# Up units in feature form: the low-weight and high-weight products issued in turns, tile by tile, instead of in two runs of eight

## The reference, cut to what matters

```python
def squared_relu_mlp(hn, w_up, w_down):
    return jnp.square(jax.nn.relu(hn @ w_up)) @ w_down
...
        h = h + squared_relu_mlp(rmsnorm(h, mlp_norm_g[i]), mlp_w_up[i], mlp_w_down[i])
...
        hf = _rms_norm(x, norm_ffn_pre[l])
        u = _dwconv_causal(hf @ w_up[l], ffn_dw[l]) + ffn_dw_b[l]
        u_g, u_v = jnp.split(u, 2, axis=-1)
        yff = (jax.nn.silu(u_g) * u_v) @ w_down[l]
```

## Time and profile before

| | |
|---|---|
| time, median of 3 runs | 1252.89 us (1252.87 to 1253.22) |
| span of the profiled execution, first to last instruction | 1249.1 us |
| median less span | 3.8 us |
| PE busy | 1220.7 us, 98% |
| PE weight loads busy (overlap PE) | 1106.9 us, 89% |
| DVE busy | 871.6 us, 70% |
| ACT busy | 700.5 us, 56% |
| narrow products L450 | 832 |
| wide products L454 | 832 |

### The profile page before, as it was taken

One profiled execution on the slowest core, in us unless ns is written; L12 is line 12 of the kernel. 1 busy time (PEld: TensorE's weight loads), 2 busy tenths in 40 slices (PEclk: granted clock), 3 DMA queues, 4 the chain that ended last, 5 costly groups with the idle time before them and its releaser, 6 DMA issues.

```text
span 1249.1 us, 21521 instructions
## 1 busy us (share of the span) xinstructions
PE 1220.7 (98%) x8583; PEld 1106.9 (89%) x8583; DVE 871.6 (70%) x1252; ACT 700.5 (56%) x1016; POOL 56.3 (5%) x102
## 2 busy tenths in 40 slices
PE   8999989999999999999999999999999999999997
PEld 7999988888888998888888999999999977888886
DVE  5888567666666656666656589998656577778876
ACT  4984555555455554554554564656454456666663
POOL 5010020000000001000000000000000010000000
PEclk9999999999999999999999999999999999999999
DMA  7671134666554654565555565354546534555561
GB/s 223 197 203 68 38 122 150 222 214 202 186 184 151 203 165 141 166 211 180 184 185 167 172 210 184 118 162 145 179 150 203 186 107 147 174 194 190 201 201 68
DMA packets 160340, 210.80 MB, mean 169 GB/s; under 512 B 5542, under 2 KB 143220, under 8 KB 160261
## 3 DMA queue, kind: packets, MB, share of 16 engines
q1 hardware_dynamic: 157315, 202.77, 50.6%
q0 software_dynamic: 1904, 6.85, 1.4%
q10 hardware_dynamic: 1042, 0.07, 0.1%
HBM read 208.62 MB, written 1.05 MB: 168 GB/s over the span
## 4 chain that ended last, share of the span: by engine, by line
PE 79%; DVE 10%; ACT 4%; issue 2%; DMA 2%; SPq 1%; POOL 1%; DVEq 0%; POOLq 0%; ACTq 0%
PE bank L369 16%; PE bank L373 16%; PE bank L372 16%; PE bank L454 15%; PE bank L450 8%; DVE wlo L305 3%; ACT whi L297 2%; PE bank L1425 2%; DMA raw<-in_dn_w_in 1%; DVE common L2582 1%; PE bank L2003 1%; PE bank L1445 1%; ACT common L753 1%; SPq L3388 1%; PE bank L2095 1%
## 5 line engine op out<-in xcount | busy, mean ns | idle before, releaser
L305 DVE TENSOR_TENSOR wlo<-raw,whi 128x2048 fp32r<-128x2048 f32 x190 | 434.9, 2291 | 203.6 <-ACT whi L297 203.3
L297 ACT ACTIVATE whi<-raw 128x2048 fp32r<-128x2048 f32 x190 | 363.3, 1913 | 145.4 <-PE bank L369 43.5
L369 PE MATMUL bank<-xparts,whi 128*128 128x256 f32 x912 | 262.5, 288 | 0.4 <-DVE common L2764 0.4
L373 PE MATMUL bank<-xparts,wlo 128*128 128x256 f32 x912 | 258.7, 284 | 0.0
L372 PE MATMUL bank<-xparts,whi 128*128 128x256 f32 x912 | 258.6, 284 | 0.0
L454 PE MATMUL bank<-xparts,whi 128*128 128x512 f32 x832 | 208.0, 392 | 0.0
L369 PEld LDWEIGHTS bank<-xparts,whi 128*128 128x128 f32 x912 | 175.5, 192 | 2.8 <-issue 2.1
L372 PEld LDWEIGHTS bank<-xparts,whi 128*128 128x128 f32 x912 | 175.6, 192 | 0.6 <-issue 0.5
L373 PEld LDWEIGHTS bank<-xparts,wlo 128*128 128x128 f32 x912 | 175.5, 192 | 0.0
L454 PEld LDWEIGHTS bank<-xparts,whi 128*128 128x128 f32 x832 | 149.8, 189 | 26.9
L369 PE MATMUL bank<-whi,hhi 128*128 128x512 f32 x392 | 153.1, 391 | 3.8 <-DVE hlo L1061 2.3
(11 more groups left out here) (391 smaller groups left out, 1706.2 us busy)
## 6 DMA issues: line engine op xcount, KB each, us to landing
raw<-in_mlp_w_up SPq DMA_DIRECT2D x32, 1024.0 KB, 5.5
raw<-in_mlp_w_down SPq DMA_DIRECT2D x32, 1024.0 KB, 5.1
raw<-in_w_in SPq DMA_DIRECT2D x22, 1024.0 KB, 5.3
raw<-in_w_up SPq DMA_DIRECT2D x22, 1024.0 KB, 5.2
raw<-in_w_gate SPq DMA_DIRECT2D x16, 1024.0 KB, 5.5
raw<-in_dn_w_in SPq DMA_DIRECT2D x15, 1024.0 KB, 5.8
raw<-in_mb_w_in SPq DMA_DIRECT2D x12, 1024.0 KB, 5.2
raw<-in_w_down SPq DMA_DIRECT2D x11, 1024.0 KB, 4.9
```

Of the source, the lines that this page charges most:

```text
L297: nc.scalar.activation(whi[:, s, :], raw[:, r, :], ACT.Copy).then_inc(hi_ready, 1)
L305: nc.vector.tensor_tensor(wlo[:, s, :], raw[:, V % RAW, :], f32(whi[:, s, :]), ALU.subtract).then_inc(lo_ready, 1)
L369: ins = pe.matmul(o, shi, mhi, start=first, stop=False, skip_group_check=True)
L373: return pe.matmul(o, slo, mhi, start=False, stop=last, skip_group_check=True)
```

## The change

One line goes, so that the loop over k that held only the narrow products now holds the wide product of the same tile too: narrow 0, wide 0, narrow 1, wide 1, and so on. The number of matmuls, of weight loads, of semaphores and of waits stays as it was. The first matmul into a bank is still the narrow product of k = 0 and the last one the wide product of k = 7. The joined branch (`if norm`) is unchanged.

```diff
@@ -481,7 +481,6 @@
                         ins = low_weights(f, k, k == 0)
                         if f == 0 and k == 0:
                             ins.then_inc(unit_begun, 1)
-                    for k in range(KT):
                         ins = high_weights(f, k, k == KT - 1)
                     ins.then_inc(uses[f].filled, 1)
                     if between and f == 0:
```

## The result

Slower. The changed kernel takes 1256.97 us (median of 4 runs, 1256.73 to 1258.49), the kernel before 1252.88 us (median of 4, 1251.36 to 1253.22), 4.1 us more. The ratio, paired run by run, is 1.0041 with a 95% interval of 1.003 to 1.0053.

A forecast was written before the change was run, and what follows sets the result against it. PE, busy 98% of the span, was taken to bound the kernel. A pair at 0.346 us makes a half 2.768, 0.025 less; 100 halves save 2.5 us: 1252.9 - 2.5 = 1250.4 us, range 1245.3 to 1255.5 us.

The forecast's parts named there:

- The present cost of a half: Three successive halves in the kernel before: 8.38 us, 2.793 us each, of which the narrow run takes 0.953.
- settled spacings: Start-to-start times in long streams of one size: 0.120 us for 256 columns, 0.2267 us for 512.
- the lower bound of a pair: Lowest time for one narrow and one wide product in turns: 0.113 + 0.2267 = 0.340 us.
- The upper bound: Highest time for a narrow and wide product in turns, both at their dearest: 0.120 + 0.233 = 0.353 us.
- PSUM at 0: Wide product adding to the columns the narrow one just added to: no new stall, taken as 0.
- the choice within the bounds: Spacing of a pair in the changed halves: taken as 0.113 + 0.233 = 0.346 us, from today's spacings behind the other kind.
- slower: each switch costs: Changed halves: each narrow product renews a slowly decaying dear state; pair 0.353 us, 3.1 us slower, 1256.0 us; chance 0.18.
- a sign that it is wrong: In the profile after, a narrow product under 0.110 us or a wide one over 0.236 would show the prediction wrong.
- The smaller term: Down units behind up units: five wide products 0.004 us too dear each, 0.02 us; some 40 units, 0.8 us.
- Both at their cheapest: Changed halves: pair 0.340 us, 7.3 us gained, 1245.6 us; chance 0.27 for gains of 3 to 7.3 us.
- Order makes no difference: Changed halves: the sum per matmul is the same in any order; half stays 2.793 us, time 1252.9 us; chance 0.11.

The follow-up runs named there:

- blocks of two: Kernel before, with each half's narrow and wide products alternating two by two; timed 1252.03 us against 1252.33, ratio 0.9999.
- blocks of three, three, two: Kernel before, with each half as three narrow, three wide, three narrow, three wide, two narrow, two wide; one run took 1250.44 us.
- blocks of four: Kernel before, with each half as four narrow, four wide, four narrow, four wide products; one run took 1253.54 us.
- wide, narrow, narrow, wide: Kernel before, with the first half of a unit running its wide run before its narrow run; 1251.27 us against 1252.61, ratio 0.9989.

## Why the prediction was wrong

**What held.** PE sets the end, and what its stream gains or loses in the 100 halves appears at the end: 3.7 us in the stages, 4.1 us in the time. No wait took it up or added to it. The present cost of a half (2.793) and the settled spacings were right, and so was the lower bound of a pair, 0.340, on which a pair of 128 and 512 columns sits. The upper bound hit the result, 0.353, by luck. It was put together from a narrow product at 0.120 and a wide one at 0.233, which is a mean of three and not the dearest (the prediction itself names 0.236 further down). In turns the narrow ones average 0.117 and the wide ones 0.237: neither term is met, and their errors cancel. PSUM at 0 was right: the order of banks is of no account.

**The step that failed** is the choice within the bounds: "I take the last, because those two rows are the nearest", 0.113 + 0.233 = 0.346 us. The runs show 0.353, the rival "slower: each switch costs", which had a chance of 0.18 and a price of 3.1 us. The two rows were read after eight of one kind. In turns only one of a kind stands before the other, and there the narrow ones average 0.117 us where the sum has 0.113, and the wide ones 0.237 where it has 0.233: both terms were mis-sized by about 0.004 us. One wide product in three takes 0.241, above the 0.236 that the prediction named as a sign that it is wrong. I took the place of a matmul in its run as all that matters, and didn't give the state that lasts for five more products, which the same rows show, the weight it had. The rival's account of that state, a slow decay that one narrow product renews, has the right price here, but two narrow products ought to renew it as well, and blocks of two have only a quarter of the extra; so its number is right and its mechanism isn't shown.

**The smaller term.** "If the end of an up unit leaves wide products dear" was put at 0.8 us and left inside the range. It came: 0.02 us a down unit. The halves' 100 x 0.03 = 3.0 us and 40 x 0.02 = 0.8 us make 3.8 us, against 3.7 in the stages, read to a tenth. Added to 1252.9 that is 1256.7 us, near the 1257.0 measured and above the range's 1255.5: the range ended short of the first part's price alone, and the second never came on top of it.

**The rivals.** "Both at their cheapest" needs one load and one wide product to be all, and that is so at 128 columns only. "Order makes no difference" is refuted by six orders of the same 32 products:

| order of a unit | switches from narrow to wide | unit, us | above settled 5.547 | first five of the down unit, above settled 1.133 |
|---|---|---|---|---|
| in turns (the change) | 16 | 5.646 | 0.099 | 0.021 |
| blocks of two | 8 | 5.573 | 0.026 | 0.000 |
| blocks of three, three, two | 6 | 5.588 | 0.041 | 0.012 |
| blocks of four | 4 | 5.608 | 0.061 | 0.025 |
| runs of eight (before) | 2 | 5.587 | 0.040 | 0.000 |
| wide, narrow, narrow, wide | 1 | 5.567 | 0.020 | 0.000 |

These are medians over the units of each trace that stand between two down units, 29 of them; from unit to unit they differ by 0.001 us.

The cost doesn't rise with the number of switches: it is lowest at one and at eight. With the down unit's part, blocks of four cost twice as much as runs of eight (0.086 against 0.040). Shown is that products in turns cost extra when their column counts differ and none when they are equal, and that the bank and the alternation of low and high weights are not the reason. The weight load isn't the reason at 384 columns; at 256, where the narrow product leaves it only 0.007 us to spare, it is excluded only as far as the extra there is the same as at 384. What in TensorE makes it, and why blocks of two are spared, stays open; the two rules that I expected for it (a fixed price for each switch, and a price by the place since the last switch) both failed at blocks of two. The 0.353 us of a pair is thus measured, and not derived from a cause.

## What to carry to other kernels

A spacing that is read right behind a switch after a long run holds for long runs only; if an edit makes the switch periodic, a state that outlasts the switch (here the five dear products) is the row to price, and the dear end of the bounds is the first candidate. Where PE is the bound and its weight loads are already hidden, mixing sizes matmul by matmul gains nothing to hide: put products of one column count beside each other, across neighbouring units too (here worth 1.3 of 1252.6 us; other sizes than these weren't tried). Compare stage by stage from start to start; whole spans of two profiles differed here by 2.5 us in code that was the same.

## What the runs showed of the hardware

- In turns, 256 and 512 columns fall into a cycle of three pairs of 1.06 us that repeats without drift; equal sizes (512 and 512) have a plain 0.2267 us. Behind the turns, five more matmuls of 512 columns take 1.154 us in place of 1.133.
- Settled spacings were 0.120 us for 256 columns and 0.2267 us for 512. The 256 columns between them take the difference, 0.1067 us, which is one column to a period of the 2.4 GHz clock; with it, each of the two carries 0.0133 us besides its columns. The Trainium skill (TensorE: Matmul & The Clock Gate, "Back-to-back issue gap") has 0.0025 us for this, in a formula that it gives for an isolated gap; here every matmul has a weight load of its own. An unequal pair carried 0.0333 (0.353 - 0.320).
- With 128 columns the wide product was recorded as begun 0.06 us after the narrow one, before the 0.113 us of a load were over, and lasted that much longer: the recorded start isn't the moment at which the weights are in place.
- The clock was at its 1.2 GHz level for part of 140 to 150 us in one profile (0.66 on average) and not in another (1.00), with PE busy for all 10 us in both, and for 9.6 of the 10 us ahead of them. The spread of the times goes with it: of the 15 executions of the kernel before that were timed beside the first experiments, those at a mean granted clock of 0.998 took 1250.8 to 1251.4 us and those at 0.995 took 1253.2 to 1253.8 us.
